# Four norms' rows of scales sent through DRAM by DMA, three norms' sums of squares by two full-width products

## The reference, cut to what matters

```python
D_MODEL, SEQ, DEPTH, D_FF, RMS_EPS = 1024, 512, 2, 2816, 1e-6

def rms_norm(x, g):
    return x * lax.rsqrt(jnp.mean(x * x, axis=-1, keepdims=True) + RMS_EPS) * g

def swiglu(x, w_in, w_out):
    gate, up = jnp.split(x @ w_in, 2, axis=-1)
    return (jax.nn.silu(gate) * up) @ w_out

def reference(x, ...):
    h = x
    for i in range(DEPTH):            # mixer 0: FoX attention; mixer 1: sliding window
        h = h + 0.5 * swiglu(rms_norm(h, norm_g[i, 0]), ffn_w_in[i, 0], ffn_w_out[i, 0])
        h = h + mixer(rms_norm(h, norm_g[i, 1]))
        h = h + 0.5 * swiglu(rms_norm(h, norm_g[i, 2]), ffn_w_in[i, 1], ffn_w_out[i, 1])
    return rms_norm(h, final_g)
```

## Time and profile before

| | |
|---|---|
| median of 3 runs | 1869.68 us (1867.63 to 1871.52) |
| the profiled execution | 1868.03 us, of which span 1866.2 us |
| granted TensorE clock in it | 0.999 of full speed |
| PE busy | 1849.2 us, 99% of the span |
| DVE / ACT busy | 926.1 us (50%) / 696.1 us (37%) |
| POOL busy | 24.7 us |
| DMA, mean over the span | 97 GB/s |

### The profile page before, as it was taken

One profiled execution on the slowest core, in us unless ns is written; L12 is line 12 of the kernel. 1 busy time (PEld: TensorE's weight loads), 2 busy tenths in 40 slices (PEclk: granted clock), 3 DMA queues, 4 the chain that ended last, 5 costly groups with the idle time before them and its releaser, 6 DMA issues.

```text
span 1866.2 us, 24031 instructions
## 1 busy us (share of the span) xinstructions
PE 1849.2 (99%) x8703; PEld 1522.8 (82%) x8703; DVE 926.1 (50%) x1337; ACT 696.1 (37%) x1149; POOL 24.7 (1%) x44
## 2 busy tenths in 40 slices
PE   9999999999999999999999999999999999999998
PEld 7888888877777888888888888888887888888888
DVE  5444434356887544444334444434379644444332
ACT  5232223245765432323323323323368433232332
POOL 1000000000000000000000000000000000000000
PEclk9999999999999999999999999999999999999999
DMA  4223223323332232222333232223322222222332
GB/s 170 101 91 101 87 89 105 119 95 107 86 94 67 94 102 91 100 97 81 110 107 106 96 101 90 96 88 108 122 79 70 91 93 98 99 92 90 96 104 84
DMA packets 59882, 181.85 MB, mean 97 GB/s; under 512 B 7472, under 2 KB 10032, under 8 KB 59824
## 3 DMA queue, kind: packets, MB, share of 16 engines
q1 hardware_dynamic: 59680, 181.05, 30.0%
q10 hardware_dynamic: 144, 0.03, 0.0%
HBM read 171.48 MB, written 2.10 MB: 93 GB/s over the span
## 4 chain that ended last, share of the span: by engine, by line
PE 94%; DVE 2%; ACT 2%; issue 1%; DMA 0%; POOL 0%; DVEq 0%; SPq 0%; ACTq 0%; POOLq 0%
PE bank L498 89%; PE bank L874 1%; PE bank L890 1%; ACT scratch L1473 0%; PE bank L906 0%; ACT wide_hi L1423 0%; DVE scratch L2019 0%; PE bank L994 0%; DVE w_lo L1546 0%; PE bank L524 0%; DVE wmax L1969 0%; ACT wide_hi L1279 0%; PE bank L565 0%; DVE wide_lo L1985 0%; DMA scratch<-x_dram 0%
## 5 line engine op out<-in xcount | busy, mean ns | idle before, releaser
L1546 DVE TENSOR_TENSOR w_lo<-raw,w_hi 128x1024 fp32r<-128x1024 f32 (+1 forms) x343 | 392.2, 1143 | 818.5 <-ACT w_hi L1114 817.4
L1114 ACT ACTIVATE w_hi<-raw 128x1024 fp32r<-128x1024 f32 (+1 forms) x343 | 341.1, 995 | 848.1 <-PE bank L498 841.4
L498 PE MATMUL bank<-u_hi,w_hi 128*128 128x512 f32 (+1 forms) x1592 | 630.3, 396 | 0.3 <-DVE w_lo L1546 0.3
L498 PE MATMUL bank<-u_hi,w_lo 128*128 128x512 f32 (+1 forms) x1592 | 620.2, 390 | 0.0
L498 PE MATMUL bank<-u_lo,w_hi 128*128 128x512 f32 (+1 forms) x1592 | 620.2, 390 | 0.0
L498 PEld LDWEIGHTS bank<-u_hi,w_lo 128*128 128x128 f32 (+1 forms) x1592 | 298.1, 187 | 63.9
L498 PEld LDWEIGHTS bank<-u_hi,w_hi 128*128 128x128 f32 (+1 forms) x1592 | 298.6, 188 | 61.0 <-issue 1.1
L498 PEld LDWEIGHTS bank<-u_lo,w_hi 128*128 128x128 f32 (+1 forms) x1592 | 298.5, 188 | 59.1 <-issue 1.0
L498 PE MATMUL bank<-wide_hi,w_hi 128*128 128x512 f32 (+1 forms) x812 | 314.7, 388 | 1.2 <-DVE w_lo L1546 1.1
L498 PE MATMUL bank<-wide_hi,w_lo 128*128 128x512 f32 (+1 forms) x812 | 313.1, 386 | 0.0
L498 PE MATMUL bank<-wide_lo,w_hi 128*128 128x512 f32 (+1 forms) x812 | 313.1, 386 | 0.0
(11 more groups left out here) (210 smaller groups left out, 1246.9 us busy)
## 6 DMA issues: line engine op xcount, KB each, us to landing
raw<-ffn_in_dram SPq DMA_DIRECT2D x175, 512.0 KB, 3.2
raw<-ffn_out_dram SPq DMA_DIRECT2D x128, 384.0 KB, 3.0
raw<-mix_w_dram SPq DMA_DIRECT2D x51, 512.0 KB, 3.2
wide_hi<-wide_hi SPq DMA_DIRECT2D x28, 128.0 KB, 2.3
y_dram<-raw SPq DMA_DIRECT2D x8, 256.0 KB, 2.7
wide_lo<-wide_lo SPq DMA_DIRECT2D x14, 128.0 KB, 2.3
wide_hi<-wide_hi SPq DMA_DIRECT2D x7, 256.0 KB, 2.8
scratch<-x_dram SPq DMA_DIRECT2D x2, 512.0 KB, 7.1
```

Source lines behind the costliest of these rows:

```text
L498: mm = pe.matmul(out, a, b, start=first and k == 0, stop=last and k == n - 1)
L1114: act.activation(w_hi[:, slot, 0:cols], raw[:, (base + r) % RAW, 0:cols], ACT.Copy)\
L1546: dve.tensor_tensor(w_lo[:, s, 0:cols], raw[:, r, 0:cols], f32(w_hi[:, s, 0:cols]), ALU.subtract).then_inc(w_ready, 1)
```

## The change

The norms 1, 2, 3 and 5 get `rstd_row` by DMA: SP writes `rstd` (128 x 4) to a row of 512 floats in DRAM in token order and, when that has landed, reads the row back with a broadcast to 128 partitions (`place_row`). PE `row_sums`, DVE `diagonals` and ACT `row_copy` remain for norms 0 and 4. In the FFN norms 2, 3 and 5 the sums over partitions are made by `square_sums`: `acc` is split into hi and lo (in a free piece of `wide_hi`/`wide_lo`), and two fp32r products with a 128 x 128 of ones put every token's sum on every partition; DVE then picks the own token by a multiplication with the identity and a reduction (`own_means`). Norm 1 (FoX) keeps `token_sums`. In FoX the forget chain moves behind the split of one more unit.

```diff
+            def place_row(nn):
+                count = 16 * ROW_MOVES[nn]
+                sp.wait_ge(rstd_ready, nn + 1)
+                sp.dma_start(row_dram.rearrange("o (t p) -> (o p) t", p=P), rstd[:, :], allow_slow_non_contiguous=True)\
+                  .then_inc(row_turned, 16)
+                sp.wait_ge(row_turned, count)
+                sp.dma_start(rstd_row[:, :], row_dram.to_broadcast([P, SEQ])).then_inc(row_placed, 16)
...
                 else:
                     load_in(0)
-                with sp.Fori(1, IN_BODIES) as i:
+                    load_in(1)
+                    place_row(nn)
+                with sp.Fori(1 if f == 0 else 2, IN_BODIES) as i:
...
+                    if u == RAW + 3:
+                        place_row(1)
...
+            def square_sums(f, nn):
+                pe.wait_ge(consts, 2)
+                pe.wait_ge(acc_lo_ready, f)
+                at = slice(SQUARES_AT, SQUARES_AT + SEQ)
+                pe.matmul(bank[5][:, :], ones_r[:, :], wide_hi[:, at], start=True, stop=False)
+                pe.matmul(bank[5][:, :], ones_r[:, :], wide_lo[:, at], start=False, stop=True).then_inc(tok_sum, 1)
...
                         if peeled and r == 1:
-                            token_sums(nn, 5)
-                        if peeled and r == 2:
-                            row_sums(nn)
+                            square_sums(f, nn)
...
                     if k == V_UNITS // 2:
-                        pe.wait_ge(row_ready, nn + 1)
+                        pe.wait_ge(ms_ready, nn + 1)
...
-                    if k == 1:
-                        row_sums(nn)
...
+                        if f and type(i) is int and r == 0:
+                            act.wait_ge(acc_ready, 9 * nn)
+                            act.activation(wide_hi[:, SQUARES_AT:SQUARES_AT + SEQ], acc[:, :], ACT.Copy)\
+                               .then_inc(acc_hi_ready, 1)
...
+            def squares_lo(f):
+                at = slice(SQUARES_AT, SQUARES_AT + SEQ)
+                dve.wait_ge(acc_hi_ready, f)
+                dve.tensor_tensor(wide_lo[:, at], acc[:, :], f32(wide_hi[:, at]), ALU.subtract)\
+                   .then_inc(acc_lo_ready, 1)
+                dve.wait_ge(acc_lo_ready, f)
+                dve.memset(acc[:, :], 0.0).then_inc(acc_ready, 1)
+
+            def own_means(f, nn):
+                dve.wait_ge(tok_sum, nn)
+                for t in range(TB):
+                    dve.scalar_tensor_tensor(out=diag[:, t * P:(t + 1) * P], in0=bank[5][:, t * P:(t + 1) * P],
+                                             scalar=1.0 / D, in1=ident[:, :], op0=ALU.mult, op1=ALU.mult)\
+                       .then_inc(own_picked, 1)
+                dve.wait_ge(own_picked, (TB + 1) * f - 1)
+                dve.tensor_reduce(ms[:, :], diag[:, :].rearrange("p (t c) -> p t c", c=P), AX_X, ALU.add)\
+                   .then_inc(own_picked, 1)
+                dve.wait_ge(own_picked, (TB + 1) * f)
+                dve.tensor_scalar(ms[:, :], ms[:, :], RMS_EPS, None, ALU.add).then_inc(ms_ready, 1)
...
+                            if first and f:
+                                dve.wait_ge(row_placed, 16 * ROW_MOVES[nn])
...
+                    if k == 1:
+                        dve.wait_ge(row_placed, 16 * ROW_MOVES[nn])
+                        dve.wait_ge(unit_used, FOX_BASE + 2)
+                        dve.tensor_tensor(x0, bank[4][0:HEADS, :], rstd_row[0:HEADS, :], ALU.mult).then_inc(f_chain, 1)
```

More of the change, by code:

```diff
@@ L46 @@
 FIRST_AT = (11264, 10240)
+ROW_MOVES = {1: 1, 2: 2, 3: 3, 5: 4}
+ROW_PRODUCTS = {0: 1, 4: 2}
 LAST_PAIR = (KB // 2 - 1) * len(OUT_KBS)
@@ L51 @@
 WO_UNITS = (KB // 2) * len(WO_KBS)
+SQUARES_AT = (FB - 1) * SEQ
 V_UNITS = 8
@@ L109, in build @@
         ones = sb("ones", [P, P])
+        ones_r = sb("ones_r", [P, P], F32R)
         ident_bf = sb("ident_bf", [P, P], BF16)
@@ L167, in build @@
         acc_ready = sem("acc_ready")
+        acc_hi_ready = sem("acc_hi_ready")
+        acc_lo_ready = sem("acc_lo_ready")
+        own_picked = sem("own_picked")
         tok_sum = sem("tok_sum")
@@ L173, in build @@
         row_ready = sem("row_ready")
+        row_turned = sem("row_turned")
+        row_placed = sem("row_placed")
         gate_scaled = sem("gate_scaled")
@@ L1192, in in_body @@
                             split_next(base + 4 * i + r + 1, base, r, i)
-                        if type(i) is int and r == 2:
+                        if f and type(i) is int and r == 0:
+                            act.wait_ge(acc_ready, 9 * nn)
+                            act.activation(wide_hi[:, SQUARES_AT:SQUARES_AT + SEQ], acc[:, :], ACT.Copy)\
+                               .then_inc(acc_hi_ready, 1)
+                        if f == 0 and type(i) is int and r == 2:
                             row_copy(nn)
@@ L1315, in fox @@
                     n += 1
-                    if k == 1:
+                    if k == 2:
                         act.wait_ge(consts, 1)
@@ L1638, in in_body @@
                                .then_inc(biases_ready, 1)
+                        if first and f and r == 0:
+                            squares_lo(f)
                         if first and r == 1:
@@ L1641, in in_body @@
                                 first_mean_squares()
+                                diagonals(nn)
                             else:
-                                mean_squares(nn, 5)
-                            diagonals(nn)
+                                own_means(f, nn)
                         if r == (2 if first else 1):
                             dve.wait_ge(unit_used, base + 4 * i + (3 if f == 0 and first else 2))
-                            if first:
-                                dve.wait_ge(row_ready, nn + 1)
+                            if first and f == 0:
+                                dve.wait_ge(row_ready, ROW_PRODUCTS[nn])
+                            if first and f:
+                                dve.wait_ge(row_placed, 16 * ROW_MOVES[nn])
                             for c in range(2):
@@ L1761, in fox @@
                 n += 1
-                diagonals(nn)
-                dve.wait_ge(row_ready, nn + 1)
-                dve.wait_ge(unit_used, FOX_BASE + 2)
-                dve.tensor_tensor(x0, bank[4][0:HEADS, :], rstd_row[0:HEADS, :], ALU.mult).then_inc(f_chain, 1)
-                dve.wait_ge(f_chain, 1)
-                dve.tensor_scalar(x0, x0, bf[:, 0:1], None, ALU.add).then_inc(f_chain, 1)
-                dve.wait_ge(f_chain, 2)
-                dve.scalar_tensor_tensor(out=x1, in0=x0, scalar=-1.0, in1=x0, op0=ALU.mult, op1=ALU.max)\
-                   .then_inc(f_chain, 1)
-                dve.tensor_scalar(x3, x0, 0.0, None, ALU.min).then_inc(f_chain, 1)
                 def project_scaled(n, is_q, count):
```

30 lines of the change are left out of this document (19 added, 11 removed).

## The result

| | before | with the change |
|---|---|---|
| median of 4 runs | 1869.79 us (1867.63 to 1871.52) | 1903.24 us (1903.01 to 1906.1) |
| ratio, 95% interval | | 1.0183 [1.0165, 1.0201] |
| profiled execution / its span | 1868.03 / 1866.2 us | 1903.01 / 1901.2 us |
| granted TensorE clock | 0.999 | 0.992 |

The account below looks back on a forecast made before the run. PE, busy 1849.2 of 1866.2 us, was taken to bound the kernel. 5.2 us saved less 1.2 us of FFN waits gave 4.0 us less: 1864.0 us profiled, 1865.7 us median; range 1863.6 to 1872.0 us.

Parts of the forecast that it names:

- PE's savings: PE sheds token_sums and row_sums for two products: 1.42 us in each of three FFNs, 0.92 in FoX, together 5.2 us.
- The chain up to the first DMA: FFN body 0: DVE's picks, reduction and addition take 2.0 us, POOL 1.01 us; SP sees the scale at 1003.9.
- The deadline: Before FFN body 1: PE does not wait if X + Y is at most 4.3 us; beyond, each microsecond costs three.
- X: The write of 512 numbers of 4 bytes to DRAM, issue to landing: 2.1 us.
- Y: The broadcast read of 256 KB from the DRAM row: 2.6 us.
- The recorded sign of being wrong: The prediction is wrong if PE waits over 1.7 us in each FFN, or if new waits appear elsewhere.
- The rival of the slow pieces: Each number is its own DRAM write; PE waits 3.5 us three times, 5.3 us more, 1875.0 us; chance 0.12.
- the 1 us of room: FoX before the q projection: bank 0 is free at 404.0, PE wants it at 405.0, so cost 0.
- rival of the late forget chain: FoX's row lands some 3 us later; 1.5 us of waiting before the q projection, 1867.2 us; chance 0.08.
- SP's queue: SP issues nothing while waiting for X; unit 8's load behind it is not delayed, cost 0.
- The rival that the transfers only eat the gain: PE waits 1.7 us per FFN at X + Y = 6.0, spending the saving; in the middle 1869.6 us; chance 0.20.
- the change does not do what it says: PE's two new products cost 0.92 us each, cutting the saving to about 1.1 us; put into the first rival.

Follow-up runs that it names:

- two versions without slow transfers: Kernel before with FFN norms' rows made without transfer: 1865.07 us; that plus FoX's row by DMA in partition order, copied to token order on DVE: 1864.1 us.
- fast-write version: The whole change with the row written in partition order, 16-byte pieces, and read by DVE with a stride: 1877.95 us against 1869.73 before, ratio 1.0038.
- held-load version: The whole change with the row in 16-byte pieces, and SP issuing unit 8's load only after the row has landed: 1872.99 us, ratio 1.0021.
- FoX alone: Kernel before with only norm 1's row by DMA in token order, its row_sums gone and the forget chain moved: 1875.79 us against 1869.14, ratio 1.0039.
- the version without a row to send: Kernel before with norms 2, 3, 5 computing the scales on every partition from the ones products, no transfer, FoX unchanged: 1865.07 us against 1869.39, ratio 0.9978.

## Why the prediction was wrong

**PE's savings: right.** The products with ones at one pitch each, 1.42 us per FFN norm, 0.92 in FoX. The two versions without slow transfers gave 4.3 and 5.0 us of the 5.2.

**The chain up to the first DMA: right.** From the last product of unit 1 to the issue of the write: 5.85 us forecast, 648.33 - 642.33 = 6.0 measured in FFN 1 and 5.7 in the other two. POOL began 0.49 us after `ms` instead of 0.15, and the picks were 0.2 us shorter.

**The deadline: right.** PE was to wait for X + Y less 4.3 us. In FFN 1, X + Y is 10.1 + 3.9 = 14.0, which gives 9.7; the wait is 9.71 us. In FFN 2 and 3, 7.9 + 5.4 and 8.0 + 5.5 give 9.0 and 9.2; the waits are 8.65 and 8.83. So the sum holds to 0.4 us, and that it fits so closely in FFN 1 is luck. The recorded sign of being wrong, over 1.7 us in each FFN, is met five times over.

**X: the step that failed.** "I take 2.1, near the store, because X moves almost nothing and finds an empty queue." Measured: 7.9 to 10.1 us. I had priced a DMA by its bytes and its queue and taken the slowest row that I had, 4.6 us, as its bound. But those rows were large pieces, or 512-byte pieces into SBUF. None wrote single numbers that adjoin in DRAM, and a bound from rows of another kind bounds nothing. With the write in 16-byte pieces, at 1.4 to 2.5 us, 25 of the 33.4 us are gone. The rival of the slow pieces named the right mechanism in part, "`row_turned` waits for the last"; its condition, X + Y over 7.3, was met by almost double, and its price of 5.3 us was too low by six times. It had 0.12 and deserved far more, since the write's pattern was the one thing in the change that the trace had never seen.

**Y: undersized.** 2.6 forecast, 3.9 to 5.5 measured: 3.0 to 3.3 for a broadcast read by itself, up to 2 us more for bytes just written in 4-byte pieces, 0.4 to 1.3 us for a load beside it.

**What was not priced: the half clock after a wait.** The bounds counted one microsecond per microsecond of waiting. Waits of 8.7 to 9.7 us in the FFNs drew 1.6 to 2.8 us of slow products behind them, and the 3.3 us in FoX 1.7 us, 7.7 us in all. Shorter waits can do it too (in the fast-write version 3.1 us ahead of 2.9 us, and 2.3 us ahead of 1.6 us) and need not (2.5 us in the same version, 2.0 us in the held-load version).

**FoX: undersized with X, and the place missed.** X + Y of 13.5 us used up the 1 us of room. The first wait came at the split of the next unit, which the change had put behind the forget chain on DVE; the prediction had followed the value banks only. Its rival of the late forget chain had the place of the smaller wait, and 1.5 us for all of FoX; alone, FoX's part costs 6.6 us.

**SP's queue: right.** The load of unit 8 was held until 659.11 and no wait of PE names it.

**The rival that the transfers only eat the gain: fell.** That "the change does not do what it says" fell too: the products are cheap.

**The top of the range** has a slip: X + Y = 6.7 gives 2.0 us more than before, 1871.7 us, not 1872.0. It changes nothing.

## What to carry to other kernels

- Price a DMA by the pattern of its writes before its bytes: 512 single 4-byte numbers side by side in DRAM took 8 to 11 us to be reported, the same bytes in 16-byte pieces 1.4 to 2.6. If no row shows a pattern, leave the range open at the top, or measure the DMA alone before building on it.
- A product with a full matrix of ones leaves the sums on every partition; where it is used, look whether the result already has the shape that the next step wants, instead of picking from it and spreading it again.
- Add to the price of a new wait of TensorE what the half clock costs behind it, here up to 3.0 us for each wait of some microseconds.

## What the runs showed of the hardware

- 512 (or 128) adjoining 4-byte writes to DRAM: 7.1 to 10.9 us to landing, of which the DMA engines were busy for some 0.7 us in the profile of the changed kernel. The 512 numbers at a distance of 32 bytes or more: 1.8 to 2.4. In 128 adjoining pieces of 8 bytes, 1 KB: 2.7 to 3.0. One piece of 2 KB: 1.15. 128 adjoining 4-byte writes to SBUF: 1.9 to 2.0. Whether the memory or the DMA's own bookkeeping makes the delay stays open.
- A broadcast of 2 KB to 128 partitions: 3.0 to 3.3 us, but 4.4 to 5.1 when these bytes were written by the slow DMA just before; write and read together then took 13.6 to 13.7 us.
- A DVE product of 128 x 512 takes 0.68 us, and 1.05 us when its SBUF operand is read with a 16-byte step; a copy of 128 x 512 that reads with this step takes 0.62 us; a reciprocal of 128 x 512 takes 3.35 us.
- After waits of 3.1 to 9.7 us the products came every 0.43 us, for 6 to 14 of them, with a granted clock of 0.50 where I read it. One wait of 3.5 us (FoX alone) was followed by full speed, and 2.1 us of waiting soon after it by 7 slow products. A wait of 2.3 us was followed by 1.0 us of full speed and then by nine slow products, one of 2.5 us by none.

Not tried: the version without a row to send for the window mixer's norm and for FoX.
